# Feed-forward layers of an fp32 two-network block: the products of the high weight part with the high and the low part of the input become one product of 512 columns

## What is computed

```python
def swiglu(h, w_gu, w_down):                 # four times, "ffn1" or "gated"
    g, u = jnp.split(h @ w_gu, 2, axis=-1)   # 1024 -> 2 x 2816
    return (jax.nn.silu(g) * u) @ w_down     # 2816 -> 1024
...
def _sq_relu_mlp(h, w1, w2):                 # four times, "ffn2" or "two-layer"
    return jnp.square(jax.nn.relu(h @ w1)) @ w2   # 1024 -> 4096 -> 1024
```

## Time and profile before

| | |
|---|---|
| median of 3 runs | 2380.91 us (2377.79 to 2382.84) |
| time of the profiled execution | 2378.58 us |
| its span | 2377.0 us |
| PE busy | 2221.3 us (93%) |
| DVE busy | 1644.3 us (69%) |
| ACT busy | 1218.7 us (51%) |
| POOL busy | 327.2 us (14%) |

### The profile page before, as it was taken

The page is one execution under the profiler, slowest core; times in us unless marked ns, Lnnn a source line. Parts: engine busy times, 40 slices in busy tenths (PEclk is TensorE's granted clock), DMA queues, the critical chain, the costliest instruction groups (busy, mean ns, idle before and its releaser), DMA issues.

```text
span 2377.0 us, 37520 instructions
## 1 busy us (share of the span) xinstructions
PE 2221.3 (93%) x14452; PEld 2031.1 (85%) x14452; DVE 1644.3 (69%) x1961; ACT 1218.7 (51%) x1911; POOL 327.2 (14%) x482
## 2 busy tenths in 40 slices
PE   2999999999999996999998999998998799998998
PEld 2998887998899795899886998987987798877987
DVE  6767764767776776776787776796766776665654
ACT  2544445544554465653464554556545554575543
POOL 0111000111121103021101120400210221000210
PEclk9999999999999998999999999999999899999999
DMA  8788883698897872797765678513788378442553
GB/s 335 249 300 292 273 295 109 239 315 288 262 322 258 310 220 72 225 324 266 259 225 189 197 262 287 174 53 99 256 288 246 91 269 282 148 135 71 180 201 106
DMA packets 296577, 532.97 MB, mean 224 GB/s; under 512 B 10097, under 2 KB 187644, under 8 KB 296444
## 3 DMA queue, kind: packets, MB, share of 16 engines
q1 hardware_dynamic: 263452, 358.05, 46.2%
q0 software_dynamic: 32992, 173.09, 20.4%
HBM read 530.00 MB, written 1.11 MB: 223 GB/s over the span
## 4 chain that ended last, share of the span: by engine, by line
PE 82%; DVE 7%; ACT 5%; issue 3%; DMA 3%; SPq 0%; POOL 0%; DVEq 0%; ACTq 0%
PE bk L1362 12%; PE bk L1363 12%; PE bk L1364 12%; PE bk L1261 9%; PE bk L1263 9%; PE bk L1262 8%; PE bk L1413 3%; PE bk L1616 2%; PE bk L1306 2%; DVE w_lo L1744 2%; DMA mod_raw<-in_ada_w 1%; PE bk L1249 1%; PE bk L1251 1%; PE bk L1250 1%; DVE mod_acc L1763 1%
## 5 line engine op out<-in xcount | busy, mean ns | idle before, releaser
L1744 DVE TENSOR_TENSOR w_lo<-raw,w_hi 128x1024 fp32r<-128x1024 f32 (+5 forms) x720 | 833.4, 1186 | 489.6 <-ACT w_hi L806 487.6
L806 ACT ACTIVATE w_hi<-raw 128x1024 fp32r<-128x1024 f32 (+5 forms) x720 | 683.3, 976 | 676.1 <-PE bk L1263 340.2
L1362 PE MATMUL bk<-a_hi,w_hi 128*128 128x256 f32 x2332 | 664.5, 285 | 5.9 <-DVE a_lo L1829 5.9
L1363 PE MATMUL bk<-a_lo,w_hi 128*128 128x256 f32 x2332 | 662.9, 284 | 0.0
L1364 PE MATMUL bk<-a_hi,w_lo 128*128 128x256 f32 x2332 | 662.8, 284 | 0.0
L1362 PEld LDWEIGHTS bk<-a_hi,w_hi 128*128 128x128 f32 x2332 | 451.0, 193 | 7.1 <-DVE a_lo L1829 4.5
L1363 PEld LDWEIGHTS bk<-a_lo,w_hi 128*128 128x128 f32 x2332 | 450.8, 193 | 0.0
L1364 PEld LDWEIGHTS bk<-a_hi,w_lo 128*128 128x128 f32 x2332 | 450.5, 193 | 0.0
L1763 DVE SCALAR_TENSOR_TENSOR mod_acc<-mod_raw,cact,mod_acc 128x1536 f32<-128x1536 f32 x182 | 329.7, 1811 | 38.1 <-DMA mod_raw<-in_ada_w 22.5
L1261 PE MATMUL bk<-w_hi,hid_hi 128*128 128x512 f32 x832 | 324.4, 390 | 3.3 <-DVE w_lo L1744 3.2
L1263 PE MATMUL bk<-w_hi,hid_lo 128*128 128x512 f32 x832 | 327.3, 393 | 0.0
(11 more groups left out here) (345 smaller groups left out, 3136.0 us busy)
## 6 DMA issues: line engine op xcount, KB each, us to landing
raw<-in_ffn_w SPq DMA_DIRECT2D x128, 1024.0 KB, 5.6
mod_raw<-in_ada_w POOLq DMA_DIRECT2D x128, 768.0 KB, 6.3
raw<-in_ffn_w_gu SPq DMA_DIRECT2D x88, 1024.0 KB, 7.4
mod_raw<-in_mod_w POOLq DMA_DIRECT2D x80, 768.0 KB, 7.0
raw<-in_ffn_w_down SPq DMA_DIRECT2D x40, 1024.0 KB, 7.1
first_mod<-in_mod_w SPq DMA_DIRECT2D x16, 768.0 KB, 9.8
raw<-in_sb_w_qkv SPq DMA_DIRECT2D x12, 1024.0 KB, 8.7
raw<-in_conv_w_pw SPq DMA_DIRECT2D x12, 1024.0 KB, 5.5
```

The lines of the kernel that those rows point to most:

```text
L806: ins = act.activation(o(w_hi[:, p % OPS, :]), r(raw[:, c % RAWS, :]), ACT.Copy)
L1362: pe.matmul(o, wh, a_hi[:, f, :], start=(f == 0), stop=False)
L1363: pe.matmul(o, wh, a_lo[:, f, :], start=False, stop=False)
L1744: ins = dve.tensor_tensor(o(w_lo[:, p % OPS, :]), r(raw[:, c % RAWS, :]), o(w_hi[:, p % OPS, :].bitcast(F32)), ALU.subtract)
```

## The change

The input's two parts now lie side by side in one tile, `a_both`, and in the eight feed-forward sublayers one matmul of 512 columns multiplies the high weights with both. Its two results land side by side in one PSUM bank: high times high in columns 0 to 255 (there the third product, low weights times high input, is added too), high times low in columns 256 to 511. They have to be added behind the product: ACT copies the upper half to `tmp`, DVE adds the lower half to it. In a gated job that gives two copies on ACT and two adds on DVE, and Silu and the product then read SBUF instead of PSUM. In a two-layer job ACT's Relu becomes a copy, DVE gets two adds, and its square becomes one operation with the Relu in it.

```diff
-        a_hi = sb("a_hi", [P, KD, S], F32R)
-        a_lo = sb("a_lo", [P, KD, S], F32R)
+        a_both = sb("a_both", [P, KD, 2, S], F32R)
+        a_hi, a_lo = a_both[:, :, 0, :], a_both[:, :, 1, :]
...
+            def split_products(w, m, f, wh, wl, wide):
+
+                o = bk[:, 4 * (w % 2) + m, :]
+                if wide:
+                    pe.matmul(o, wh, both(f), start=(f == 0), stop=False, skip_group_check=True)
+                else:
+                    pe.matmul(o[:, 0:S], wh, a_hi[:, f, :], start=(f == 0), stop=False)
+                    pe.matmul(o[:, 0:S], wh, a_lo[:, f, :], start=False, stop=False)
+                return pe.matmul(o[:, 0:S], wl, a_hi[:, f, :], start=False, stop=(f == KD - 1), skip_group_check=wide)
...
-                    def gated(w, slot, pair, i=0):
-                        act.activation(sig[:, slot, :, :], job_banks(w, 2), ACT.Silu).then_inc(sig_ready, 1)
-                        is_read(act, w, i)
+                    def gated(w, c, slot, pair, i=0):
+                        is_done(act, c - 1, i)
+                        act.activation(low_of(slot, 0), half(w, 0, 1), ACT.Copy).then_inc(low_out, 1)
+                        act.wait_ge(gate_sum, n + pair + 1)
+                        act.activation(sig[:, slot, :, :], sig[:, slot, :, :], ACT.Silu).then_inc(sig_ready, 1)
+                        is_done(act, c, i)
+                        act.activation(low_of(slot, 2), half(w, 2, 1), ACT.Copy).then_inc(low_out, 1)
+                        act.wait_ge(prod_ready, n + pair + 1)
                         act.activation(hid_hi[:, tiles(pair, 2), :], ev[:, slot, :, :], ACT.Copy)\
                             .then_inc(hhi_ready, 1)
...
                             for e in range(2):
-                                dve.wait_ge(sig_ready, n + 2 * b + e + 1 + 4 * i)
+                                dve.wait_ge(low_out, lows + 2 * b + e + 1 + 4 * i)
+                                dve.tensor_tensor(sig[:, e, :, :], half(w + b, 2 * e, 0), low_of(b, 2 * e), ALU.add).then_inc(gate_sum, 1)
+                                dve.wait_ge(gate_sum, n + 2 * b + e + 1 + 4 * i)
+                                if e:
+                                    dve.sem_inc(bank_free[(w + b) % 2], 1)
                                 dve.wait_ge(hid_ready, n + 2 * b + e + 1 + 4 * i)
-                                dve.tensor_tensor(ev[:, e, :, :], sig[:, e, :, :], sig[:, e, :, :], ALU.mult)\
-                                    .then_inc(bank_free[(w + b) % 2] if e else prod_ready, 1)
+                                dve.scalar_tensor_tensor(out=ev[:, e, :, :], in0=sig[:, e, :, :], scalar=0.0, in1=sig[:, e, :, :],
+                                                         op0=ALU.max, op1=ALU.mult).then_inc(prod_ready, 1)
...
+                    def gate_added(w, slot, pair):
+
+                        dve.wait_ge(low_out, lows + 2 * pair + 1)
+                        dve.tensor_tensor(sig[:, slot, :, :], half(w, 0, 0), low_of(slot, 0), ALU.add).then_inc(gate_sum, 1)
+
+                    def product(w, slot, n, pair):
+
+                        dve.wait_ge(low_out, lows + 2 * pair + 2)
+                        dve.wait_ge(hid_ready, n + 1)
+                        dve.tensor_tensor(ev[:, slot, :, :], half(w, 2, 0), low_of(slot, 2), ALU.add).then_inc(up_sum, 1)
+                        dve.wait_ge(up_sum, ups + n + 1)
+                        dve.sem_inc(bank_free[w % 2], 1)
                         dve.wait_ge(sig_ready, n + 1)
-                        dve.wait_ge(hid_ready, n + 1)
-                        dve.tensor_tensor(ev[:, slot, :, :], sig[:, slot, :, :], job_banks(w)[:, 2:4, :], ALU.mult)\
-                            .then_inc(bank_free[w % 2], 1)
+                        dve.tensor_tensor(ev[:, slot, :, :], ev[:, slot, :, :], sig[:, slot, :, :], ALU.mult).then_inc(prod_ready, 1)
...
                             for h in range(2):
                                 pieces(p + 4 + 4 * b + 2 * h, p + 6 + 4 * b + 2 * h, i)
                                 mod_add(st["groups"][0], 2 * i + b, h)
-                            product(w + b, c + 2 + 2 * b, b, n + 2 * i + b, i)
+                                if h == 0:
+                                    gate_added(w + b, b, 2 * i + b)
+                            product(w + b, b, n + 2 * i + b, 2 * i + b)
```

More of the change, by code:

```diff
@@ L475, in job_banks, with half, low_of, both @@
             return bk[:, 4 * (w % 2):4 * (w % 2) + n, 0:width]
+        def half(w, a, h):
+            return bk[:, 4 * (w % 2) + a:4 * (w % 2) + a + 2, S * h:S * h + S]
+        def low_of(slot, a):
+            return tmp[:, 4 * slot + a:4 * slot + a + 2, :]
+        def both(f):
+            return a_both[:, f, :, :].rearrange("p h s -> p (h s)")
         def turned_x(w, j):
@@ L1331, in first_gate_up @@
                         if f == 0:
-                            first_feature([(job_banks(w)[:, m, :], *(z[:, (p + m // 2 * 2) % OPS, P * (m % 2):P * (m % 2) + P]
-                                                                     for z in (w_hi, w_lo))) for m in range(4)], act_from)
+                            first_feature([(out_of(w, m, wide), *(z[:, (p + m // 2 * 2) % OPS, P * (m % 2):P * (m % 2) + P]
+                                                                for z in (w_hi, w_lo))) for m in range(4)], act_from, wide)
                             continue
@@ L1353, in gate_up @@
                         if act_from is not None and q == 0 and f == 0:
-                            first_feature([(job_banks(w)[:, m, :], *(z[:, p % OPS, P * m:P * m + P] for z in (w_hi, w_lo)))
-                                           for m in range(2)], act_from)
+                            first_feature([(out_of(w, m, wide), *(z[:, p % OPS, P * m:P * m + P] for z in (w_hi, w_lo)))
+                                           for m in range(2)], act_from, wide)
                             continue
```

71 lines of the change are left out of this document (34 added, 37 removed).

## The result

The changed kernel took 2444.94 us (median of 4 runs, 2438.87 to 2448.24), the kernel before beside it 2379.48 us (2377.79 to 2382.84). The ratio is 1.0285, 95% interval 1.0265 to 1.0304: slower, by 65 us where 39 were forecast. It lies at the very end of the forecast's own range (2395 to 2445 us) and also in that of rival 5 (2433 to 2465), so the total doesn't tell the two apart; the rows and experiment 1 do. The profiled execution took 2448.24 us, its span is 2446.6 us, against 2377.0 before: 69.6 us to be found.

What follows compares the result with a forecast made beforehand. PE was taken as the bound, with the DVE-ACT loop 0.14 us a job behind and becoming the bound. +40 us in gated sublayers and -1 in two-layer ones made +39: 2420 us, range 2375 to 2450, the forecast's own 2395 to 2445.

Steps and rivals of the forecast that it cites:

- rival 5: Gated jobs: PE's idling drops its clock for 3.4 us a job, +0.3 to 1 us each; 2433 to 2465 us, chance 0.08.
- What bounds the kernel: Gated first halves: PE needs 11.52 us a job, the closed DVE-ACT loop 11.38 us, leaving 0.14 us of room.
- What the change takes off PE: Feed-forward products: 0.348 instead of 0.360 us a feature, 2432 features, at most 29 us saved; a job needs 11.14 us.
- rival 2: The pair of products saves next to nothing and DVE hides its adds: 2366 to 2381 us, chance 0.05.
- What it adds in a gated job: Two DVE adds, together 1.33 us, ACT's copies free: loop 12.23 us, 13.19 with the table reload, mean 12.71.
- The walk through one gated sublayer: Job by job from PE's first product: fifth down piece 10.1 us later than before; +10 us a gated sublayer, +40 for four.
- 8.2 us as before: Gated sublayer, half way into job 8: `mod_sum` keeps its length of 8.2 us, after a PE wait of 2.5 us.
- In the down half ... nothing more is lost: Gated down half: a piece lasts PE 2.7 us, DVE needs 1.14 us and half a `mod_add`, so no further loss.
- Two-layer sublayers: Two-layer jobs: DVE's chain 11.3 to 11.7 us; three sublayers +0.7 us each, the last -3 us, together -1 us.
- The total: Whole kernel: +39 us, 2420 us; forecast's own range 2395 to 2445 us, chance 0.66.

Runs made afterwards that it cites:

- experiment 1: The changed kernel with the wide product issued as two products of 256 columns, all copies and adds kept: 2447.11 us, ratio 1.030.
- experiment 2: The changed kernel with the wide product but the old operations behind it, no adds, high weights times low input left out: 2360.24 us, ratio 0.993.
- experiment 3: The changed kernel without the gate tiles' copy and add, Silu reading the lower half in PSUM: 2404.79 us, ratio 1.011.
- experiment 4: The changed kernel with ACT making next pieces ahead of `hid_hi`: one piece 2421.67 us; two, gated only, 2405.15 us. Two in the kernel before: 2398.07 us.

## Why the prediction was right, and where its size was off

- **What bounds the kernel**: right. The loop of VectorE and ScalarE at 11.38 us was the limit that mattered; experiment 2 shows it most plainly, since without any add the gated sublayers gain nothing. My expectation for that kernel forgot my own number.
- **What the change takes off PE**: 0.012 us a feature forecast, 0.010 measured; the direction was right and rival 2 wrong. The gap formula of the Trainium skill's page "TensorE: Matmul & The Clock Gate", section "Back-to-back issue gap", would by estimate give 0.0025 us; rows of both kernels stand against it (0.120 and 0.228 us alone, 0.117 and 0.233 us in the pair).
- **What it adds in a gated job**: 12.23 and 13.19 us forecast, 12.27 and 13.32 measured. The gate add cost 0.60, the up add with its wait 0.83 (122.90 to 123.73) instead of 0.73: the wait for VectorE's own result is 0.15 us, not 0.05. ScalarE's copies cost nothing in the loop, as forecast, but VectorE did idle ahead of the gate add in jobs 0 and 10, which the prediction had named as a sign that they matter.
- **The walk through one gated sublayer** is the term that was mis-sized: "the fifth down piece comes 10.1 us later" should have been 14.9. Its start was wrong: the first multiplication at 18.1, where even the old product stood at 18.4 to 19.2 and the new one at 20.0 to 22.4; that is 3 us, of which the walk had left 2 in the range. It had left them to the wrong sublayers: in the two with four-tile order the new multiplication came only 1.1 and 1.6 us after where the old product had stood, in the other two 2.7 and 3.3 us, for there VectorE waited over 3 us for ScalarE's first copy. The seven loops from there cost 0.5 us more than forecast (88.96 against 88.49 us). The remaining 1.3 us lie at `mod_sum`. "8.2 us as before" was taken from the slowest of four (7.2 us in the mean), and it became 8.8 in the mean, with the clock falling earlier in it; the wait ahead of it was 2.0 us in the mean, 2.5 forecast. From job 7 to the fifth down piece the walk lost 2.6 us more against before, and the run 3.9.
- **"In the down half ... nothing more is lost"**: right to 0.7 us a sublayer in the number (14.9 us late at job 10, 15.6 us at the end), and that is luck, for two errors cancel. The walk took the piece's lateness for TensorE's, but TensorE had 3.0 us in hand: it started the fifth down piece only 11.9 us later than before. And from there to the end it lost 3.7 us, at pieces behind a `mod_add` that waits for its data and at the lower clock, neither of which the walk had; it looked only at VectorE's and TensorE's times a piece.
- **Two-layer sublayers**: +0.7, +0.7, +0.7 and -3 us forecast, +1.3, +1.1, +1.4 and -1.7 measured. The last sublayer's first half is 1.7 us shorter without any adds too (experiment 2), so they aren't what keeps it from 3. Squares of two jobs are 11.4 us apart (1423.12 to 1434.54), or 12.1 where a load of `mod_raw` is late:

```profile
1413.43 5.16 DVE L1769 TENSOR_TENSOR w_lo<-raw,w_hi 128x1024 fp32r<-128x1024 f32 x4 [1.76 <-ACT w_hi L821]
1419.22 1.82 DVE L1788 SCALAR_TENSOR_TENSOR mod_acc<-mod_raw,cact,mod_acc 128x1536 f32<-128x1536 f32 x1 [0.63 <-DMA mod_raw<-in_ada_w]
...
1423.12 0.69 DVE L2000 SCALAR_TENSOR_TENSOR ev<-sig 128x512 f32<-128x512 f32 x1 [0.15 <-DVE sig L1995]
...
1434.54 0.69 DVE L2000 SCALAR_TENSOR_TENSOR ev<-sig 128x512 f32<-128x512 f32 x1 [0.15 <-DVE sig L1995]
```

- **Rival 5, the clock**: partly true. It wanted a spell of 3.4 us at the lower level in each job; there were six in jobs 1 to 7 of the four sublayers, and the multiplications are 12.3 and 13.3 us apart with and without them, so they cost the first halves nothing that can be seen. It has a share in `mod_sum` (1.6 us longer each) and in two down halves (some 1.6 us each). My estimate from these rows is 10 of the 65 us; the rival had it at 13 us or more.
- **The total**: 2444.94 us is inside the forecast's own range by 0.06 us, with single runs from 2438.87 to 2448.24 us on both sides of its end. That it came out inside is luck. What speaks for the forecast are its loops and experiments 1, 3 and 4.

The sum: 4 x 15.6 us = 62.5 in gated sublayers against 40 forecast, +2.1 against -1 in two-layer ones, and +5.0 us in sublayers that weren't changed, of the size by which builds differ there.

## What to carry to other kernels

Before work is moved from TensorE to the other engines, measure the closed loop (here product, rounding, next piece, next product) from one instruction to its next copy: at 77% busy VectorE had 0.14 us a job to spare. Ask the same of the stretch that follows. Where TensorE has no idle time (here 60.2 of 61.4 us in the down half) no wait is made good, so what counts is how far its pieces are ahead of it (3.0 us here) and what stands ahead of the later ones in the other engines' programs; here a `mod_add` whose data came late, also in the versions that had opened the loop. Removing TensorE's fixed cost a product is worth 0.010 us for each product saved; one VectorE add of 0.6 us for each 32 features undoes it twice over.
